# Six of the twelve modulation groups of layer 1 moved from the context attention to the slots of the first context search

## What is computed

```python
for l in range(DEPTH):
    mod = silu(c) @ w_mod[l] + b_mod[l]          # (6 * 1024), for the latent tokens
    mod_c = silu(c_ctx) @ w_mod[l] + b_mod[l]    # the same for the context tokens
    h, hc = modulated rms_norm of x and xc
    lat, con = project_heads(h), project_heads(hc)
    x = x + gt1 * merge_branches(lat, three attentions of lat over lat and con)
    x = x + gt2 * peer_ffn(h2, wq, keys, u, v)
    if not last:
        xc = xc + gt1c * merge_branches(con, context_attention(con) ...)
        xc = xc + gt2c * peer_ffn(h2c, ...)
```

## Time and profile before

| | us |
|---|---|
| median of three runs | 2979.59 (2975.24 to 2987.22) |
| profiled execution | 2984.41 |
| its span, first to last instruction | 2982.6 |
| TensorE busy | 2324.6 (78%) |
| VectorE busy | 1786.4 (60%) |
| ScalarE busy | 1174.4 (39%) |
| GpSimd busy | 866.7 (29%) |
| gather slots | 3 x 256 |

### The profile page before, as it was taken

One profiled execution on the slowest core, in us unless ns is written; L12 is line 12 of the kernel. 1 busy time (PEld: TensorE's weight loads), 2 busy tenths in 40 slices (PEclk: granted clock), 3 DMA queues, 4 the chain that ended last, 5 costly groups with the idle time before them and its releaser, 6 DMA issues.

```text
span 2982.6 us, 32781 instructions
## 1 busy us (share of the span) xinstructions
PE 2324.6 (78%) x11156; PEld 1344.5 (45%) x11156; DVE 1786.4 (60%) x4445; ACT 1174.4 (39%) x3336; POOL 866.7 (29%) x794
## 2 busy tenths in 40 slices
PE   5999998877779988956559888887998856555555
PEld 3787897433336644612115555423788511111111
DVE  3328654785665556358876555443665777776554
ACT  4215533344653334334443343333433433433333
POOL 0000001332223334334444333342000444444442
PEclk8999999888989999967879999998999986777887
DMA  7631245999999999989999999996413999999997
GB/s 277 226 127 51 85 170 200 421 370 404 421 421 404 421 421 413 421 348 417 421 421 414 419 412 418 421 421 265 183 58 127 412 421 421 421 417 417 420 422 297
DMA packets 145383, 1017.59 MB, mean 341 GB/s; under 512 B 16064, under 2 KB 21312, under 8 KB 22720
## 3 DMA queue, kind: packets, MB, share of 16 engines
q0 software_dynamic: 112032, 810.08, 65.9%
q1 hardware_dynamic: 29440, 199.59, 17.1%
q10 hardware_dynamic: 3744, 5.83, 0.5%
HBM read 1011.25 MB, written 4.19 MB: 340 GB/s over the span
## 4 chain that ended last, share of the span: by engine, by line
PE 45%; DMA 30%; DVE 13%; ACT 6%; POOL 3%; issue 3%; ACTq 0%; POOLq 0%; SPq 0%; DVEq 0%
DMA att<-experts_in,att 28%; PE ps L1361 13%; DVE att L2627 6%; PE ps L1218 4%; POOL att L2008 3%; PE ps L658 3%; PE ps L659 3%; PE ps L660 3%; DMA ring<-stream_in 2%; PE ps L987 2%; PE ps L841 2%; PE ps L1280 2%; PE ps L811 1%; PE ps L953 1%; PE ps L1056 1%
## 5 line engine op out<-in xcount | busy, mean ns | idle before, releaser
L1361 PE MATMUL ps<-att 128*64 128x512 f32 x3072 | 955.4, 755 | 568.9 <-ACT att L1792 568.8
L2008 POOL DMA_INDIRECT att<-experts_in,att x768 | 853.8, 1112 | 1696.2 <-PE ps L1361 1173.0
L2627 DVE CUSTOM_DVE_ANT_0 att<-att 128x1024 f32<-128x1024 f32 x768 | 931.6, 1224 | 624.4 <-DMA att<-experts_in,att 614.2
L1361 PEld LDWEIGHTS ps<-att 128*64 128x64 f32 x3072 | 221.3, 160 | 1171.6 <-ACT att L1792 814.9
L1785 ACT ACTIVATE att<-att 128x1 f32<-128x1 f32 x768 | 154.2, 201 | 939.8 <-DVE att L2627 936.5
L1792 ACT ACTIVATE att<-const,att 128x64 f32<-128x64 f32 x768 | 267.0, 348 | 74.2 <-ACT att L1787 4.4
L1787 ACT ACTIVATE att<-att 128x1 f32<-128x1 f32 x768 | 226.1, 294 | 24.9
L2061 DVE TENSOR_TENSOR ring_lo<-ring,wt_hi 128x2048 fp32r<-128x2048 f32 x41 | 94.0, 2292 | 177.9 <-ACT wt_hi L1475 177.9
L1475 ACT ACTIVATE wt_hi<-ring 128x2048 fp32r<-128x2048 f32 x41 | 78.3, 1910 | 163.5 <-DMA ring<-stream_in 104.8
L658 PE MATMUL ps<-h,wt_hi 128*128 128x256 f32 (+1 forms) x360 | 113.1, 314 | 17.5 <-DVE ring_lo L2061 9.2
L659 PE MATMUL ps<-h,wt_hi 128*128 128x256 f32 (+1 forms) x360 | 111.0, 308 | 0.0
(11 more groups left out here) (270 smaller groups left out, 3387.6 us busy)
## 6 DMA issues: line engine op xcount, KB each, us to landing
ring<-stream_in SPq DMA_DIRECT2D x183, 1024.0 KB
att<-experts_in,att POOLq DMA_INDIRECT x768
att<-bias_in POOLq DMA_DIRECT2D x16, 256.0 KB, 2.9
spare<-stream_in SPq DMA_DIRECT2D x3, 1024.0 KB
gate_store<-att ACTq DMA_DIRECT2D x24, 128.0 KB, 8.1
x<-x_in ACTq DMA_DIRECT2D x1, 2048.0 KB, 8.3
att<-gate_store SPq DMA_DIRECT2D x1, 2048.0 KB, 11.4
att<-gate_store SPq DMA_DIRECT2D x1, 1024.0 KB, 13.5
```

The source lines that it names most:

```text
L1361: last = mm(ps[HALF * s:HALF * (s + 1), d, :], diag[:, (m + s) % DIAGS, :], rows[:, (m + s) % SLOTS, D + 512 * d:D + 512 * (d + 1)], start ...
L2008: nc.gpsimd.indirect_dma_start(out=rows[:, m % SLOTS, :], out_offset=None, in_=experts_in, in_offset=bass.IndirectOffsetOnAxis(ap=index[:, ...
L2627: v.tensor_tensor_reduce(out=u_row, in0=u_row, in1=dup[:, n // HK, n % 2, :], scale=1.0, scalar=0.0, op0=ALU.mult, op1=ALU.add, accum_out= ...
```

## The change

The first six of the groups stay in the attention, one in every second head. The other six go behind the expert queries of the context, into a new generator `last_groups` on TensorE and ScalarE that runs along the ticks of the first search and four ticks beyond. The pairs of these six groups are loaded behind the query weights. In the new place ScalarE copies the columns. The slots of pass 0 are dealt out anew: everything starts one slot later, the context attention gets 34 slots and not 42, the queries 26 (25), the merge 62 (59), the output projection 18 (17), the first search 14 (11), and nine slots follow for the last four ticks. A wait is added ahead of one key tile of pass 1 that uses bank 6.

```diff
+MOD_CTX = 6
+MOD_TICKS = 2 * (MOD_GROUPS - MOD_CTX) + 2
...
-TOKENS_AT = [spread(1, (REST_UNIT_TICKS, 28)) + spread(31, (SCALE_TICKS, 8), (CTX_Q_TICKS, 25), (ATTENTION_TICKS, 42), (HEAD_TICKS, 7), (MERGE_TICKS, 59),
-                    (UPDATE_TICKS, 4), (WOUT_TICKS, 17), (NORM_TICKS, 9), (WQ_TICKS, 29), (TOK_TICKS, 3), (FIRST_TICKS, 11)),
+TOKENS_AT = [spread(1, (REST_UNIT_TICKS, 28)) + spread(32, (SCALE_TICKS, 8), (CTX_Q_TICKS, 26), (ATTENTION_TICKS, 34), (HEAD_TICKS, 7), (MERGE_TICKS, 62),
+                    (UPDATE_TICKS, 4), (WOUT_TICKS, 18), (NORM_TICKS, 9), (WQ_TICKS, 29), (TOK_TICKS, 3), (FIRST_TICKS, 14),
+                    (MOD_TICKS - FIRST_TICKS, 9)),
...
-    run(MOD_PAIRS, "mod")
+    run(2 * MOD_CTX, "mod")
     MERGE_AT.append(run(MERGE_PAIRS, "raw", again=merge))
     WOUT_AT.append(run(WOUT_PAIRS, "raw", again=merge + MERGE_PAIRS))
     WQ_AT.append(run(WQ_PAIRS, "raw", again=queries))
+    run(MOD_PAIRS - 2 * MOD_CTX, "mod")
...
+                if r == 1 and tt == 0 and g == 2:
+                    pe.wait_ge(mod_cols_copied, len(MOD_PARTS) + MOD_GROUPS)
...
+            def last_groups():
+
+                for k in range(MOD_TICKS):
+                    if k % 2 == 0:
+                        g = MOD_CTX + k // 2
+                        if g > MOD_CTX:
+                            pe.wait_ge(mod_cols_copied, len(MOD_PARTS) + g - 1)
+                            second_columns(g - 1)
+                        if g < MOD_GROUPS:
+                            second_group(g)
+                    yield
...
-                    second_columns(u)
+                    if u % 2 == 0:
+                        second_columns(u // 2)
...
-                        if 0 <= k // 2 - 1 < MOD_GROUPS:
-                            second_group(k // 2 - 1)
+                        if k % 4 == 2 and k // 4 < MOD_CTX:
+                            second_group(k // 4)
...
                 key_tile(1, 0, 0)
-                yield from idle(FIRST_TICKS)
+                yield from last_groups()
...
+            def last_groups():
+
+                for k in range(MOD_TICKS):
+                    if k % 2 == 1:
+                        g = MOD_CTX + k // 2
+                        if g < MOD_GROUPS:
+                            second_row(g)
+                        if g > MOD_CTX:
+                            act.wait_ge(mod_cols_done, len(MOD_PARTS) + g)
+                            nc.scalar.activation(mod_raw[:, 4 * (g - 1):4 * g, :],
+                                                 ps[:, 6, N_LAT:N_LAT + 8].rearrange("p (u s) -> p u s", s=2), ACT.Copy)\
+                                .then_inc(mod_cols_copied, 1)
+                    yield
...
-                        if 0 <= k // 2 - 1 < MOD_GROUPS:
-                            second_row(k // 2 - 1)
+                        if k % 4 == 3 and k // 4 < MOD_CTX:
+                            second_row(k // 4)
...
-                    v.tensor_copy(mod_raw[:, 4 * u:4 * u + 4, :], ps[:, 6, N_LAT:N_LAT + 8].rearrange("p (u s) -> p u s", s=2))\
-                        .then_inc(mod_cols_copied, 1)
+                    if u % 2 == 0:
+                        v.tensor_copy(mod_raw[:, 2 * u:2 * u + 4, :], ps[:, 6, N_LAT:N_LAT + 8].rearrange("p (u s) -> p u s", s=2))\
+                            .then_inc(mod_cols_copied, 1)
```

More of the change, by code:

```diff
@@ L1107, in context_query, with second_columns, second_group @@
                 yield
+            def second_columns(g):
+                pe.wait_ge(mod_row_copied, MOD_GROUPS + g + 1)
+                for u in range(4):
+                    at = N_LAT + 2 * u
+                    last = mm(ps[:, 6, at:at + 2], mod_row[:, g % 2, tile_of(u)], sel, start=True, stop=True)
+                last.then_inc(mod_cols_done, 1)
+            def second_group(g):
+                if g:
+                    pe.wait_ge(mod_row_copied, MOD_GROUPS + g)
+                for pair in range(2):
+                    mod_pair(MOD_GROUPS + g, pair, 7)
+            def last_groups():
[8 more added lines that the diff above has]
+                    yield
             def context_attention():
@@ L1154, in values @@
                     last.then_inc(y_done, 1)
[L1156 to L1167, removed]
                 pe.wait_ge(sides_found, 8)
@@ L1835, in context_query, with second_row @@
                     yield
+            def second_row(g):
+                act.wait_ge(mod_group_done, MOD_GROUPS + g + 1)
+                if g >= 2:
+                    act.wait_ge(mod_cols_done, len(MOD_PARTS) + g - 1)
+                nc.scalar.activation(mod_row[:, g % 2, :], ps[:, 7, :], ACT.Copy).then_inc(mod_row_copied, 1)
+            def last_groups():
[10 more added lines that the diff above has]
+                    yield
             def context_attention():
@@ L1860, in copy_probt @@
                         .then_inc(probt_copied, 1)
[L1862 to L1866, removed]
                 for k in range(ATTENTION_TICKS):
@@ L1921, in behind_lat @@
                 yield from tokens(1, 0)
-                yield from idle(1 + SIDE_TICKS)
-                yield from pick_ticks(1, 0)
+                rows_of_kinds = last_groups()
+                for work in (idle(1 + SIDE_TICKS), pick_ticks(1, 0)):
+                    for _ in work:
+                        next(rows_of_kinds)
+                        yield
+                yield from rows_of_kinds
             def behind_ctx():
@@ L2687, in behind_lat @@
                 yield from picks_of(1, 0, 0)
+                yield from idle(MOD_TICKS - FIRST_TICKS)
             def behind_ctx():
```

## The result

| | before | after |
|---|---|---|
| median | 2977.9 us | 3012.5 us |
| ratio of the two on the same chip | | 1.0085 (95%: 1.0068 to 1.0102) |
| profiled execution, span | 2984.4, 2982.6 | 3013.0, 3011.0 |
| pass 0, first dot of slot 0 to that of slot 255 | 510.0 to 1340.7: 830.6 us | 514.4 to 1368.6: 854.2 us |

The forecast was 2976 us, 3.5 us faster, in a range that ended at 2991. The kernel became about 25 us slower by the ratio; the two medians of the table lie 34.6 us apart and the two profiled executions 28.4. Of the 28.4 us between the spans 23.6 lie in pass 0 and 4.4 ahead of it, where the change touches nothing; passes 1 and 2 take the same time to about 1 us each. So the question is pass 0 alone.

The account below looks back on a forecast made before the run. The DMA engines at 420 GB/s were taken to bound pass 0, so only their rest could change: -7.8 us at the end and +4.3 in the attention, -3.5 from 2979.6, gave 2976 us, range 2966 to 2991.

Parts of the forecast that it names:

- Bytes over 420 GB/s plus the rest: Pass 0: time is bytes at 420 GB/s plus the DMA engines' rest, 16.6 us before; only the rest can change.
- The hole: End of pass 0, 1297 to 1304 us: DMA share 0.15, 6.0 us of rest, mostly to be covered by moved loads.
- A gain of 7.8 us: End of pass 0: moved loads cut DMA rest from 9.8 us to 2, with ends at 0 and 9.8.
- A wait of TensorE for a pair: Last slots of pass 0: TensorE waiting for a weight pair to land, costed at nothing, end a few us.
- Its own length without transfers: Context attention if transfers were free: between 102 and 140 us, middle 121, 6 over the transfers' 115.
- TensorE's removed groups stand on the chain: Context attention: the argument against rival (a), that the groups taken out lie on the stage's chain.
- the slots were priced at 3.3 us each: Context attention: eight slots fewer, removed in series, take 8 x 3.30 = 26.4 us off its length.
- rival (c): Context attention: TensorE's clock falls to 0.68, the stage lasts some 135 us, sum +10, 2990 us; chance 0.06.
- rival (a): Context attention, slots 66 to 100: bound by its heads, 133 us long, rests 18, sum +8.5, 2988 us; chance 0.23.
- the two ends that it was built on: Context attention: DMA rest after the change forecast at 6 us, with ends 0 and 25.
- The page's sum: Context attention: with about 1.38 us of drain per table switch, ScalarE needs 125 us, 10 over the transfers.
- the forecast's 6: Context attention: DMA rest goes from 1.7 to 6 us, a loss of 4.3 us.

Follow-up runs that it names:

- e2: The kernel before with all twelve groups kept in the attention, but the changed kernel's slots (34 there): attention 152 us, ratio 0.9997 to the kernel before.
- e1: The changed kernel with the six groups moved but the old slots (42 in the attention): attention 158 us, ratio 1.0034 to the kernel before.
- e8: The changed kernel plus four unused matmuls in each of the six heads that lost their group: attention 154 us, ratio 1.0055 to the kernel before.
- e3: The changed kernel plus eight unused matmuls in each of the six heads that lost their group: attention 143 us, ratio 1.0051 to the kernel before.
- e9: The changed kernel with its six remaining groups in heads 0 to 5, not every second head: attention 145 us, ratio 1.0035 to the kernel before.
- e7: The changed kernel plus sixteen unused matmuls in each of the six heads that lost their group: attention 150 us, ratio 1.0034 to the kernel before.
- e4: The changed kernel with tanh in place of gelu, so no table loads in the attention (wrong activation): attention 136 us, ratio 1.0011 to the kernel before.

## Why the prediction was wrong

**Right: what bounds the pass.** "Bytes over 420 GB/s plus the rest" held. The bytes are the same, and the change of the unmoved time in two stages, +23.2 us, is pass 0's to 0.4 us; the other stages changed by about nothing, as forecast. Pass 1 didn't pay for the loads at its edge: 718.5 us from its first dot to its last, for 717.7. The merge took 196.6 us for the forecast 200, full.

**Right: the end.** A gain of 7.8 us was forecast from the busy share, with 9.8 as the end of its range. By the share 9.8 came, since it is 1.01 throughout; by the bytes it is 11.5. The hole is gone. A wait of TensorE for a pair, which the prediction named as a sign of error and costed "at nothing; the end is a few us", did come, once. TensorE's timeline of the kernel after (start, duration in us; in brackets the idle time ahead of it and what ended it):

```profile
1321.56 1.94 PE L674 MATMUL ps<-ring,cond 128*32 128x512 f32 x8 [3.07 <-DMA ring<-stream_in]
```

3.07 us, while the DMA engines stood at 1.01, as the window of the end above has it: it cost TensorE's time and no transfer, and nothing of the pass.

**Wrong: the attention.** Its own length without transfers was put between 102 and 140 us, with 121 taken. It is 159. Three parts of that step failed.

First, both ends took the removed instructions off the length, the lower one in series, the upper one TensorE's part. Next to nothing came off. A group lies for the most part in TensorE's wait beside the ring, not on it: with all twelve, in 34 slots, the stage takes 152 us (e2). The argument that TensorE's removed groups stand on the chain was a misreading. In the earlier trace rows the group's product has 3.3%, 5.6 us of the 23.1 that it is busy: a chain that is mostly compute was taken for a series of all that is computed. It is compute for more than the 39% suggest, since inside the window the gather's transfer has 27%.

Second, the slots were priced at 3.3 us each. 42 or 34 make next to no difference: 158 us in e1 for 159 at a better clock (0.82 for 0.77), and 123.2 us of heads for 123.5 in e8 at like clock. The gather's steps are part of the ring, and a round has one pair of slots in it or a pair is done between rounds. The time of the stage is then, as an estimate, the number of rounds by their length. The 29 ticks are 14.5 heads' worth, at 9.6 us 139 and at 12.1 us 175, and 143 (e3) and 159 lie between these.

Third, the clock. It stood as rival (c) with 0.06, at +10 us. By the windows of e3 and e9 it made 13 to 16 of the 34.7 us more that the attention left unmoved, by the ratios of e3, e7 and e9 10 to 15 us of the kernel. The rest, some 18 to 22 us, is the ring at its better clock, which is rival (a): it was given 18 us of rest at 133 us of length, and 0.23. The rest came near this price, the length did not (143 to 145). Neither case reaches the result alone, and the error in the odds was to let them stand beside each other as separate ones. Here they came together: with the groups gone from every second head TensorE waits longer in the ring, and work put into these waits brought the clock back (e3, e7, e8). The rule of the Trainium skill named there ("TensorE: Matmul & The Clock Gate", "Part 1: The HAM clock gate"), that only activity lifts the clock, agrees with these runs: 1.00 over the 51 us with a group in each head, 0.79 in the heads without (e9).

**The range.** It stopped at 2991, although the two ends that it was built on gave up to +25 us in the attention. With that end added it would have reached some 3005, still 8 us short of the median.

**The table load.** The sum went by the row, 1283 ns and no drain behind it, against the page of the Trainium skill, "ScalarE: Activation LUTs", "What ACT_TABLE_LOAD costs". e4 took 24 us from the stage, 31 from ScalarE's busy time, with all 24 of its table loads gone: 31.2 / 24 = 1.3 us each, as the row has it. A drain would be idle time, and the chain of the kernel after has 0.01 us before the load at 798.13 and as little behind it. The count was wrong: the earlier trace rows has the loads of two lines, and with those of L1845 (3) and L1771 (2) there were 26 in the stage before, not 21. The page's sum, 10 us over the transfers, came a little nearer to the result than the forecast's 6, but not by its reason.

## What to carry to other kernels

Before work is taken out of a stage that waits in a ring through several engines, find one round of that ring in the chain in order of time, and take off only what stands in it; what lies in an engine's wait gives next to nothing back. Count the chain's entries only inside the window before their shares are read. Work in TensorE's waits can be what holds its clock up: if some of it must go, leave what remains in neighbouring rounds and not in every second one, and allow for products on the ring that take twice as long. And where transfers are the limit, a stage that loses loads must get other transfers in their place, not fewer slots.

## What was not expected of the hardware

The same products, in consecutive heads or in every second one, gave a granted clock of 1.00 or of 0.80 over the same 51 us (e9 and the kernel after); work whose result nobody uses (11.5 us on TensorE) shortened a stage by 16.

The DMA busy share flatters a stage that is not full. In the attention after it reads 0.83 of 1.01, which would be 345 GB/s, where 321 were moved. By the share 29 us weren't used, by the bytes 37.5, and the bytes make pass 0's sum come out. So it is before: by the share 16.6 us of pass 0 weren't used, by the bytes (1 - 406 / 420) x 831 = 27.7. A prediction by shares is best repeated with GB/s.
